# Moving the weight remainders from VectorE to GpSimd in a two-layer hybrid decoder

## The reference

```python
ada = c_act @ w_ada[l] + b_ada[l]                     # shifts, scales, gates
h = rms_norm(x, norm1_g[l]) * (1.0 + sc1) + sh1
z, xbc, dt_raw, q, k, v, gate_s, gate_a = split_cols(h @ w_in[l], IN_PROJ_WIDTHS)
y_ssm = mamba2_branch(z, xbc, dt_raw, ...) @ w_ssm_out[l]
y_att = diff_attention_branch(q, k, v, ...) @ w_attn_out[l]
mixed = sigmoid(gate_s) * y_ssm + sigmoid(gate_a) * y_att
x = x + g1 * (mixed @ w_out[l])
h = rms_norm(x, norm2_g[l]) * (1.0 + sc2) + sh2
x = x + g2 * (square(relu(h @ w_ff1[l])) @ w_ff2[l])
```

## Time and profile before

| | |
|---|---|
| median of 3 runs (lowest, highest) | 3022.24 us (3013.09, 3028.65) |
| profiled execution: time, span | 3028.65 us, 3026.7 us |
| mean granted TensorE clock | 0.912 |
| busy: TensorE, VectorE, ScalarE, GpSimd | 2584.0, 1500.0, 960.4, 133.7 us |
| read from HBM | 244.0 MB |

### The profile page before, as it was taken

The page is one execution under the profiler, slowest core; times in us unless marked ns, Lnnn a source line. Parts: engine busy times, 40 slices in busy tenths (PEclk is TensorE's granted clock), DMA queues, the critical chain, the costliest instruction groups (busy, mean ns, idle before and its releaser), DMA issues.

```text
span 3026.7 us, 35812 instructions
## 1 busy us (share of the span) xinstructions
PE 2584.0 (85%) x12200; PEld 2058.5 (68%) x12200; DVE 1500.0 (50%) x2195; ACT 960.4 (32%) x1532; POOL 133.7 (4%) x121
## 2 busy tenths in 40 slices
PE   5798889889777698999978988888897767799997
PEld 2586667787665476888736866687776655678885
DVE  5775444444555345333367754544455553453333
ACT  1244332333444223222213443322334442232221
POOL 0001130000000000000000012200000000000000
PEclk9898889899999698999988998988899977899998
DMA  7421011122111121222273211012121111212221
GB/s 305 166 97 56 28 55 44 68 83 87 46 43 42 43 95 72 95 95 93 100 293 112 97 42 55 28 58 82 55 104 42 42 42 56 84 70 97 97 97 56
DMA packets 34518, 251.58 MB, mean 83 GB/s; under 512 B 3824, under 2 KB 4208, under 8 KB 4976
## 3 DMA queue, kind: packets, MB, share of 16 engines
q1 hardware_dynamic: 34416, 250.30, 22.6%
HBM read 244.00 MB, written 6.29 MB: 83 GB/s over the span
## 4 chain that ended last, share of the span: by engine, by line
issue 72%; PE 17%; DVE 4%; DMA 2%; DVEq 1%; POOL 1%; ACT 1%; POOLq 1%; PEldq 0%; PEld 0%; ACTq 0%; SPq 0%
PE gemm L384 3%; PE gemm L385 3%; PE gemm L386 3%; DMA raw<-stream 2%; PE aux L448 2%; PE aux L525 2%; POOL smalls L1515 1%; PE aux L516 1%; DVE decayed L1252 1%; PE aux L535 1%; PE aux L416 1%; DVE conv L1194 0%; DVEq L1291 0%; DVE y_tok L1292 0%; DVE seg L1242 0%
## 5 line engine op out<-in xcount | busy, mean ns | idle before, releaser
L1102 DVE TENSOR_TENSOR w_lo<-raw,w_hi 128x2048 fp32r<-128x2048 f32 x176 | 405.1, 2303 | 628.2 <-ACT w_hi L732 620.5
L384 PE MATMUL gemm<-h_hi,w_hi 128*128 128x512 f32 x1536 | 650.7, 424 | 34.6 <-DVE h_lo L1466 11.5
L732 ACT ACTIVATE w_hi<-raw 128x2048 fp32r<-128x2048 f32 x176 | 336.6, 1914 | 905.1 <-PE gemm L386 802.2
L385 PE MATMUL gemm<-h_lo,w_hi 128*128 128x512 f32 x1536 | 616.9, 402 | 0.0
L386 PE MATMUL gemm<-h_hi,w_lo 128*128 128x512 f32 x1536 | 615.1, 400 | 0.0
L384 PEld LDWEIGHTS gemm<-h_hi,w_hi 128*128 128x128 f32 x1536 | 299.7, 195 | 134.6 <-issue 60.1
L384 PE MATMUL gemm<-op_hi,w_hi 128*128 128x512 f32 x896 | 357.7, 399 | 12.6 <-ACT zh L897 9.0
L385 PE MATMUL gemm<-op_lo,w_hi 128*128 128x512 f32 x896 | 355.1, 396 | 0.0
L386 PE MATMUL gemm<-op_hi,w_lo 128*128 128x512 f32 x896 | 354.7, 396 | 0.0
L385 PEld LDWEIGHTS gemm<-h_lo,w_hi 128*128 128x128 f32 x1536 | 299.7, 195 | 71.0 <-issue 12.9
L386 PEld LDWEIGHTS gemm<-h_hi,w_lo 128*128 128x128 f32 x1536 | 299.5, 195 | 65.9
(11 more groups left out here) (171 smaller groups left out, 2791.2 us busy)
## 6 DMA issues: line engine op xcount, KB each, us to landing
raw<-stream SPq DMA_DIRECT2D x200, 1024.0 KB, 4.8
ada_raw<-stream SPq DMA_DIRECT2D x24, 1024.0 KB, 7.5
xsave<-x SPq DMA_DIRECT2D x2, 2048.0 KB, 12.5
x<-xsave SPq DMA_DIRECT2D x2, 2048.0 KB, 7.7
x<-xT SPq DMA_DIRECT2D x1, 2048.0 KB, 7.5
out<-y_out SPq DMA_DIRECT2D x1, 2048.0 KB, 6.3
dtw_raw<-dtw SPq DMA_DIRECT2D x2, 512.0 KB, 8.0
rope_cos<-ropes SPq DMA_DIRECT2D x2, 256.0 KB, 2.8
```

What stands on the lines that cost most here:

```text
L384: mm(o, w_hi[:, slot, k, cols], hi[:, k, :], start=k == 0, stop=False)
L385: mm(o, w_hi[:, slot, k, cols], lo[:, k, :], start=False, stop=False)
L732: A(w_hi[:, slot], raw[:, slot], ACT.Copy).then_inc(hi_ready, 1)
L1102: TT(w_lo[:, slot], raw[:, slot], w_hi[:, slot].bitcast(F32), ALU.subtract).then_inc(lo_ready, 1)
```

## The change

`low` becomes an instruction of GpSimd. All 88 per layer are taken out of VectorE's program and put into GpSimd's, in the same order of units; the operation, its operands and its semaphores are the same. VectorE's feed-forward rounds become one loop of four again. ScalarE's, TensorE's and SP's programs are as before.

```diff
-            def low(l, nh, slot):
-                dve.wait_ge(hi_ready, l * UNITS + nh * 2 + (slot + 1))
-                TT(w_lo[:, slot], raw[:, slot], w_hi[:, slot].bitcast(F32), ALU.subtract).then_inc(lo_ready, 1)
...
                     def gate_y(u):
-                        low(l, i * 4 + (U_ZS // 2 + u // 2 + 1), u % 2)
                         for j in range(2):
...
-                    if pair + 1 < PAIRS and n % (2 * TB) in (2, 5, 7):
-                        low_qkv(pair + 1, n % (2 * TB) // 3)
...
+            def low(l, nh, slot):
+                pool.wait_ge(hi_ready, l * UNITS + nh * 2 + (slot + 1))
+                gp.tensor_tensor(w_lo[:, slot], raw[:, slot], w_hi[:, slot].bitcast(F32), ALU.subtract)\
+                    .then_inc(lo_ready, 1)
...
                 rsqrt(ms, rs, st, "ms", "rs")
+                low(l, 0, 0)
+                low(l, 0, 1)
+                with pool.Fori(1, U_GATE // 2 + 1) as i:
+                    low(l, i, 0)
+                    low(l, i, 1)
                 with pool.Fori(0, GROUPS) as g:
...
                     pool.drain().then_inc(S_["dx"], 1)
+                    low(l, g + (U_GATE // 2 + 1), 0)
+                    low(l, g + (U_GATE // 2 + 1), 1)
                 with pool.Fori(0, 2) as i:
                     st = Step(l, "z", i)
                     for gg in range(2):
+                        for slot in range(2):
+                            low(l, i * 4 + (U_ZS // 2 + gg + 1), slot)
                         rsqrt(y_ms, y_rs, st, "y_ms", "y_rs")
+                    for u in range(4):
+                        low(l, i * 4 + (U_ZS // 2 + 3 + u // 2), u % 2)
...
+                for n, (pair, h, j) in enumerate(ATT):
+                    if n and n % TB == 0:
+                        rsqrt(y_ms, y_rs, st, "o_ms", "o_rs")
+                    if pair + 1 < PAIRS and n % (2 * TB) in (2, 5, 7):
+                        low_qkv(pair + 1, n % (2 * TB) // 3)
+                rsqrt(y_ms, y_rs, st, "o_ms", "o_rs")
                 st = Step(l, "mix")
+                for nh in range(U_AO // 2 + 1, U_FF // 2 + 1):
+                    low(l, nh, 0)
+                    low(l, nh, 1)
                 rsqrt(ms, rs, st, "ms", "rs")
+                with pool.Fori(U_FF // 2 + 1, UNITS_H) as i:
+                    low(l, i, 0)
+                    low(l, i, 1)
```

More of the change, by code:

```diff
@@ L1423, in o_low @@
                     dve.drain().then_inc(S_["o_lo"], 1)
[L1425 to L1429, removed]
                 rope(0, 0)
-                low_qkv(0, 1)
                 rope(0, 1)
-                low_qkv(0, 2)
                 maxima(0)
@@ L1472, in dve_program @@
                             ALU.mult, ALU.add).then_inc(bank_free[u % 2], 1)
-                    if u < N_WO - 1:
-                        low(l, U_WO // 2 + 1 + u // 2, u % 2)
                 dve.drain().then_inc(S_["x_sum"], 1)
-                low(l, U_WO // 2 + 1 + (N_WO - 1) // 2, (N_WO - 1) % 2)
                 norm_sums(st)
                 norm(st, lambda k: amul[:, KB + k:KB + k + 1], lambda k: ada_v[:, 3, k:k + 1])
-                def ff_round(i, last_round):
+                with dve.Fori(0, 4) as i:
                     sf = Step(l, "ff", i)
                     for u in range(4):
-                        low(l, i * 4 + (U_FF // 2 + u // 2 + 1), u % 2)
                         for j in range(2):
@@ L1493, in ff_round @@
                     for u in range(4):
-                        if u < 2 or not last_round:
-                            low(l, i * 4 + (U_FF // 2 + 2 + u // 2 + 1), u % 2)
                         for j in range(2):
@@ L1500, in ff_round @@
                     settle()
-                with dve.Fori(0, 3) as i:
-                    ff_round(i, False)
-                ff_round(3, True)
                 dve.drain().then_inc(S_["layer"], 1)
@@ L1553, in pool_program, with low_qkv @@
                     for gg in range(2):
+                        for slot in range(2):
+                            low(l, i * 4 + (U_ZS // 2 + gg + 1), slot)
                         rsqrt(y_ms, y_rs, st, "y_ms", "y_rs")
+                    for u in range(4):
+                        low(l, i * 4 + (U_ZS // 2 + 3 + u // 2), u % 2)
                 st = Step(l, "att")
-                for head in range(AH):
-                    rsqrt(y_ms, y_rs, st, "o_ms", "o_rs")
+                def low_qkv(pair, u):
+                    n = 3 * pair + u
+                    low(l, U_QKV // 2 + n // 2 + 1, n % 2)
+                for u in range(3):
+                    low_qkv(0, u)
+                for n, (pair, h, j) in enumerate(ATT):
[4 more added lines that the diff above has]
+                rsqrt(y_ms, y_rs, st, "o_ms", "o_rs")
                 st = Step(l, "mix")
+                for nh in range(U_AO // 2 + 1, U_FF // 2 + 1):
+                    low(l, nh, 0)
+                    low(l, nh, 1)
                 rsqrt(ms, rs, st, "ms", "rs")
+                with pool.Fori(U_FF // 2 + 1, UNITS_H) as i:
+                    low(l, i, 0)
+                    low(l, i, 1)
             rsqrt(ms, rs, Step(DEPTH, "start"), "ms", "rs")
```

13 lines of the change are left out of this document (removed).

## The result

The changed kernel takes 3045.2 us (median of 4 runs, 3040.8 to 3049.1) against 3023.3 us for the kernel before, measured beside it: a ratio of 1.0081, 95% interval 1.0058 to 1.0104. It is slower by 0.8%. The forecast was 2991 us with a range up to 3035, so both the sign and the range were missed.

What follows compares the result with a forecast made beforehand. Feed-forward was taken as TensorE-bound, so only waits in the state-space, z and attention stages and handovers between stages could change the time; terms summed to -31 us, giving 2991 us from the 3022.24 median, range 2925 to 3035.

Steps and rivals of the forecast that it cites:

- Part 6: Attention: VectorE's difference and rope no longer queue behind `low`, so TensorE waits less: -38 us, between -8 and -60.
- Part 5: z stage: VectorE's all-SBUF gates behind `low` held 1.9 us longer, three a round on TensorE's path: +23 us.
- part 3: State-space groups: the 2.00 us wait for a decayed tile goes in all 8, -16 us; late xdt and small holds +2.
- Part 4: State-space clock: part of the low granted clock after that wait goes, -10 us, between 0 and -35.
- Parts 1, 2, 7 and 8: Layer opening +4 us, end of xs -3, merge and second norm +7, feed-forward 0.
- Part 8: Feed-forward: u_lo held 1.9 us longer stays hidden by 0.2 us, so 0; cover gone beyond a `low` of 4.4 us.
- A: Rival: long GpSimd and VectorE instructions interleave, nothing is held; 2923 us, chance 0.10.
- B: Rival: holding as forecast, but the clock stays up in state-space groups and attention; 2946 us, chance 0.18.
- C: Rival: attention loops over ScalarE and VectorE, so next waits replace those gone; attention -19, total 3020 us, chance 0.20.
- D: Rival: slower, since a `low` on GpSimd really takes about 6.1 us; +56, 3078 us, chance 0.12.

Runs made afterwards that it cites:

- z_gate_dve: Changed kernel with only the z stage's first four w_lo of a round (gate units) back on VectorE: 3007.1 us, ratio 0.9945 to the kernel before.
- ssd_only: Kernel before with only the state-space groups' w_lo on GpSimd: 3007.0 us, ratio 0.9948.
- quarters: Changed kernel with every w_lo as four GpSimd instructions of 128x512: 3000.6 us, ratio 0.9934 to the kernel before.
- att_ts: Changed kernel with the scaling of attention's maxima split into two 128x1 instructions: 3019.5 us, ratio 0.9992 to the kernel before.

## Why the prediction was wrong

**Part 6 is the step that failed, with the rule that it rested on.** "A VectorE instruction with two SBUF operands can't run beside a `low` on GpSimd, and one that reads PSUM can" left open the third kind, one SBUF operand, and the argument went on as if that were free. `maxima` ends in such an instruction. With it split, attention gains 39 us over both layers, of which 33.5 are idle time, for the -38 forecast. That is an agreement of sums and not of terms: TensorE's waits for a p fell from 84.6 to 43.9 us (23 were forecast), those for rope only from 27.1 to 23.9 (14 were forecast), and its waits for the exponentials' probs grew from 16.0 to 25.7, which no term had. With the instruction whole these three are 50.3, 32.3 and 30.7, and attention gains 17.5. Those 21 us are more than half of the 35 by which z and attention miss.

**Part 5 had the mechanism and was mis-sized.** Three gates a round held by the longer instruction: shown. But a `low` takes 4.64 us, so each costs 4.64 - 2.30 = 2.34 instead of 1.9: 28 us in place of 23, and 31 by z_gate_dve. The part omitted what it did work out for the feed-forward stage: when the weights themselves are ready. Among the half units a slot's next w_lo is needed some 5.5 us after its last use; at the fourth wait above, conversion took 1.92 us and the subtraction 4.87, and with the hand-overs w_lo came 1.6 us late. Once a round, that is 6.5 us in all, some 5 by the stages.

**Parts 3 and 4 had their own terms about right and left one out.** The 2.0 us wait went in all eight groups: the -16. What was added back is 0.5 us a group, +4 and not +2, and not by a late xdt but by the held addition in front of the fifth tile; part 3 had that `low` over before it could hold anything that counts. At full clock a group's eight tiles take 38.8 us before and 37.2 after, -13 for eight. Part 4's low clock behind the wait went too: 40.2 - 38.8 = 1.4 us a group, 11 in all, for the -10, though a single fall cost 2.7 us at the most and not up to 5; in part that is the shorter waits for the seventh and eighth tile. The term left out is the clock between the groups, 2.3 us longer in the mean, six times. So the stage's -21.4 in the two profiles lies near the -24 by luck in part: in the mean of all profiles it is -13.5, and ssd_only gives 16 us, 11 to 21, for the kernel.

**Parts 1, 2, 7 and 8** were right in sign or nearly nothing: +4.5 for +4, -1.9 for -3, +9.8 for +7 (in part again 4.6 us in place of 4.2), and +2.3 for 0. Part 8 said that the cover is gone at a `low` of 4.4 us: 8 x (4.64 - 4.4) = 1.9 us by its own rule. A feed-forward round in the middle of the stage takes 87.45 us after, 87.04 before and in quarters; TensorE has no idle time there that would name the wait.

**The rivals.** A (nothing is held) is refuted by the 4.09 and 3.81 us rows, B and C by the sign. C's attention of -19 is near the measured -17.5, but by another way: att_ts shows that the hold took the rest, not the loop over ScalarE and VectorE. D had the right side by way of a 6.1 us `low`; the longest is 5.0. What it shared with the truth is that the hold, longer than assumed, decides. With the measured values in its terms (parts 3 and 4 at -21, part 5 at +38, part 6 at -18, part 7 at +10, part 8 at +2, the others as forecast) the same sum is 4 - 3 - 21 + 38 - 18 + 10 + 2 = +12, of 15 in the profiles: it was complete in form but for the late weights and the clock between the groups, and its sign hung on how long one instruction takes and which others it holds.

## What to carry to other kernels

Moving a long instruction from VectorE to GpSimd does not free VectorE for its duration: list every VectorE instruction in its shadow by its kind of operands, the tiny ones on the path to another engine first, since a hold costs the same whether the held instruction takes 0.17 or 0.69 us. Cut the long GpSimd instruction or leave it where VectorE's next work must wait for it anyway; here choosing by stage gained 1.7% where moving all lost 0.8%. And before pricing a stage from one profile, split its length into idle and busy with the clock beside it, look at the same stage of another layer, and compare one repeated piece of it at the same clock: where the clock is low some waits shrink, so the idle time alone can hide what was won.

## What the runs showed of the hardware

A VectorE tensor_scalar of 128x2 from SBUF to SBUF is held to the end of a running GpSimd tensor_tensor (up to 4.43 us instead of 0.17); the 128x1 form never was (longest 0.155 us of 128 in att_ts, 36 of them beside a GpSimd subtraction). A VectorE copy of 128x512 with one SBUF operand was held too (4.31 us instead of 0.42). GpSimd's 128x2048 subtraction takes 4.50 us at the least and 4.61 in the median; four of 128x512 take 5.2 us. The state-space stage, unchanged, took 205.8 to 219.3 us in ten instances with its idle time within 23.7 to 25.6: TensorE's granted clock, 0.87 to 0.95 there, moved it by more than most of the terms of the forecast. Behind a 2.0 us wait of TensorE the mean clock of the next 10 us was between 0.52 and 0.83 in 27 of 40 groups; without that wait it was 1.00 in all 72.
